# Reordering three engines inside a step of the second block's neighbourhood attention, and moving TensorE's fill to the step's end

## The reference, cut to what matters

```python
proj = h @ w_in[l]
q_lat, kv_lat, k_pe, g_mla, na_q, na_k, na_v, g_na = jnp.split(proj, split_at, axis=-1)
y_mla = _mla(...) * jax.nn.silu(g_mla)
y_na  = _na(na_q, na_k, na_v, ...) * jax.nn.silu(g_na)
h_res = h_res + jnp.concatenate([y_mla, y_na], axis=-1) @ w_out[l]
```

```python
s = concatenate([q k^T * scale + rel_bias (in the window), q k_meta^T * scale + meta_bias])
o = softmax(s) @ [v_win, v_meta]
```

## Time and profile before

| | us |
|---|---|
| median of 3 runs | 1332.66 (1331.65 to 1333.54) |
| the profiled execution, whole | 1332.1 |
| its span, first to last instruction | 1330.3 |
| TensorE matmul busy | 1257.1 (94% of the span) |
| VectorE / ScalarE / Pool busy | 822.6 / 658.1 / 152.2 |

### The profile page before, as it was taken

The page is one execution under the profiler, slowest core; times in us unless marked ns, Lnnn a source line. Parts: engine busy times, 40 slices in busy tenths (PEclk is TensorE's granted clock), DMA queues, the critical chain, the costliest instruction groups (busy, mean ns, idle before and its releaser), DMA issues.

```text
span 1330.3 us, 27430 instructions
## 1 busy us (share of the span) xinstructions
PE 1257.1 (94%) x10074; PEld 1208.1 (91%) x10074; DVE 822.6 (62%) x1378; ACT 658.1 (49%) x1105; POOL 152.2 (11%) x209
## 2 busy tenths in 40 slices
PE   6999999999999999999999999999799999976778
PEld 6999999999999999999999999999698799765667
DVE  6666655777666656666557776676666654343334
ACT  5554544455445444445445554554466566243332
POOL 3000001440000000000104400000200000043310
PEclk9999999999999999999999999999899999998888
DMA  7555644345556535556443465565244124332221
GB/s 276 190 187 191 233 162 148 124 143 200 180 188 227 191 125 185 189 189 230 165 153 123 147 197 177 186 229 185 104 138 136 49 95 151 125 109 77 95 80 64
DMA packets 56197, 210.89 MB, mean 159 GB/s; under 512 B 6672, under 2 KB 8720, under 8 KB 56000
## 3 DMA queue, kind: packets, MB, share of 16 engines
q1 hardware_dynamic: 54048, 203.45, 45.5%
q0 software_dynamic: 1936, 6.47, 1.5%
q10 hardware_dynamic: 144, 0.06, 0.0%
HBM read 208.91 MB, written 1.05 MB: 158 GB/s over the span
## 4 chain that ended last, share of the span: by engine, by line
PE 88%; DVE 5%; ACT 3%; issue 2%; DMA 0%; DVEq 0%; ACTq 0%; SPq 0%
PE bank L1056 26%; PE bank L1058 25%; PE bank L1057 25%; DVE w_lo L668 2%; PE bank L1381 2%; PE bank L1094 2%; ACT w_hi L402 2%; PE bank L1364 1%; DVE h_lo L687 1%; ACT probs_T L625 1%; PE bank L1292 1%; PE bank L1294 1%; PE bank L1293 1%; PE bank L1346 1%; PE bank L1149 0%
## 5 line engine op out<-in xcount | busy, mean ns | idle before, releaser
L1056 PE MATMUL bank<-h_hi,w_hi 128*128 128x256 f32 (+1 forms) x1992 | 573.5, 288 | 32.8 <-DVE silu_all L906 16.1
L1057 PE MATMUL bank<-h_lo,w_hi 128*128 128x256 f32 (+1 forms) x1992 | 566.6, 284 | 0.0
L668 DVE TENSOR_TENSOR w_lo<-w_raw,w_hi 128x1024 fp32r<-128x1024 f32 (+1 forms) x360 | 466.3, 1297 | 161.8 <-ACT w_hi L402 161.0
L1058 PE MATMUL bank<-h_hi,w_lo 128*128 128x256 f32 (+1 forms) x1992 | 566.2, 284 | 0.0
L402 ACT ACTIVATE w_hi<-w_raw 128x1024 fp32r<-128x1024 f32 (+1 forms) x360 | 397.8, 1109 | 94.2 <-PE bank L1058 69.9
L1056 PEld LDWEIGHTS bank<-h_hi,w_hi 128*128 128x128 f32 x1992 | 381.6, 192 | 43.1 <-issue 38.9
L1058 PEld LDWEIGHTS bank<-h_hi,w_lo 128*128 128x128 f32 x1992 | 382.7, 192 | 0.0
L1057 PEld LDWEIGHTS bank<-h_lo,w_hi 128*128 128x128 f32 x1992 | 380.0, 191 | 0.9
L1056 PE MATMUL bank<-g_hi,w_hi 128*128 128x256 f32 x832 | 230.4, 277 | 0.8 <-DVE x_res L853 0.8
L1057 PE MATMUL bank<-g_lo,w_hi 128*128 128x256 f32 x832 | 229.8, 276 | 0.0
L1058 PE MATMUL bank<-g_hi,w_lo 128*128 128x256 f32 x832 | 229.7, 276 | 0.0
(11 more groups left out here) (153 smaller groups left out, 1217.5 us busy)
## 6 DMA issues: line engine op xcount, KB each, us to landing
w_raw<-in_w SPq DMA_DIRECT2D x296, 512.0 KB, 3.3
w_raw<-in_wd SPq DMA_DIRECT2D x64, 704.0 KB, 4.1
rel_bias<-in_relbias POOLq DMA_DIRECT2D x32, 128.0 KB, 2.3
btab_sb<-in_btab POOLq DMA_DIRECT2D x1, 1536.0 KB, 10.3
x_res<-in_xT SPq DMA_DIRECT2D x2, 512.0 KB, 5.0
out_T<-x_res SPq DMA_DIRECT2D x8, 128.0 KB, 1.7
rope_sb<-in_rope POOLq DMA_DIRECT2D x1, 272.0 KB, 3.7
mats_sb<-in_mats POOLq DMA_DIRECT2D x1, 192.0 KB, 3.9
```

What stands on the lines that cost most here:

```text
L668: dve.tensor_tensor(wlo[:, slot, 0:cols], raw[:, slot, 0:cols], whi[:, slot, 0:cols].bitcast(F32), ALU.subtract).then_inc(lo_ready[slot], 1)
L1056: pe.matmul(o, h, xh, start=first, stop=False)
L1057: pe.matmul(o, h, xl, start=False, stop=False)
L1058: return pe.matmul(o, lo, xh, start=False, stop=last)
```

## The change

TensorE's step becomes scores(i), values(i-2), transposes(i-1), fill(i): the fill comes last. ScalarE's probs_T moves from behind exp(i), where it was for step i-1, to the start of step i, where it is for step i-2. VectorE makes the `w_lo` of piece i+2 in step i instead of that of piece i+3, from step 1 on. Pool issues the two DMAs of a step first, then makes both copies, then both waits and additions. The number and the sizes of all instructions stay the same, and so does the first attention's order.

```diff
-            for i in range(2 * NH):
-                h, t = 2 * (i // 4) + i % 2, i // 2 % 2
-                if i >= 4:
-                    pool.wait_ge(nm_done, U0 + 2 * MH + i - 3)
-                pool.dma_start(rel[:, i % 4, 0:T], relbias[h][:, 2 - 2 * t:6 - 2 * t, :].rearrange("p r c -> p (r c)"))\
-                    .then_inc(rel_loaded[i % 4], 16)
-                pool.tensor_copy(rel[:, i % 4, T:TM], metab[:, h, :])
-                pool.wait_ge(rel_loaded[i % 4], 16 * (i // 4 + 1))
-                r4 = rel[:, i % 4, 0:T].rearrange("p (r c) -> p r c", r=4)
-                pool.tensor_tensor(r4, r4, cmask[:].unsqueeze(1).broadcast_to([P, 4, GW]), ALU.add).then_inc(rel_ready, 1)
+            for step in range(NH):
+                t = step % 2
+                for hh in range(2):
+                    i, h = 2 * step + hh, 2 * (step // 2) + hh
+                    if step >= 2:
+                        pool.wait_ge(nm_done, U0 + 2 * MH + i - 3)
+                    pool.dma_start(rel[:, i % 4, 0:T], relbias[h][:, 2 - 2 * t:6 - 2 * t, :].rearrange("p r c -> p (r c)"))\
+                        .then_inc(rel_loaded[i % 4], 16)
+                for hh in range(2):
+                    pool.tensor_copy(rel[:, (2 * step + hh) % 4, T:TM], metab[:, 2 * (step // 2) + hh, :])
+                for hh in range(2):
+                    i = 2 * step + hh
+                    pool.wait_ge(rel_loaded[i % 4], 16 * (i // 4 + 1))
+                    r4 = rel[:, i % 4, 0:T].rearrange("p (r c) -> p r c", r=4)
+                    pool.tensor_tensor(r4, r4, cmask[:].unsqueeze(1).broadcast_to([P, 4, GW]), ALU.add)\
+                        .then_inc(rel_ready, 1)
...
             def attention(v0, steps, mla):
                 for i in range(steps + 3):
+                    if not mla and 2 <= i < steps + 2:
+                        probs_T(v0, i - 2)
...
-                    if 1 <= i <= steps:
+                    if mla and 1 <= i <= steps:
                         probs_T(v0, i - 1)
...
-                    if not mla and i < FILL:
-                        split2(FILL0 + i + LEAD)
+                    if not mla and 1 <= i <= FILL:
+                        split2(FILL0 + i - 1 + LEAD)
...
                     if i < steps:
                         scores(v0, i, mla)
-                        if not mla:
-                            fill(i)
                     if i >= 2:
                         values_of(v0, i - 2, mla)
                     if 1 <= i <= steps:
                         transposes(v0, i - 1)
+                    if i < steps and not mla:
+                        fill(i)
```

## The result

The changed kernel takes 1277.53 us (median of 4, 1277.10 to 1277.77), the kernel before 1332.16 beside it. The ratio is 0.9589, with a 95% interval of 0.9573 to 0.9606. The forecast was 1283 us with a range of 1276 to 1295. The profiled execution took 1277.69 us with a span of 1275.9, 54.4 us less than the one of before; 49.9 were forecast.

What follows compares the result with a forecast made beforehand. No engine was full; a loop of waits through TensorE, ScalarE and VectorE set the pace. Work 83.8 plus stalls 6.6 gives 90.4 for 138.9, saving 48.5, plus 1.4 in the tail: 49.9, so 1283 us (1276 to 1295).

Steps and rivals of the forecast that it cites:

- The loop: In the 16 steps, a loop of waits sets the pace; 37.2 us of gaps before fills go.
- The new stall behind the tanh: Steps 2 to 8: values wait for probs_T queued behind the tanh, 0.70 or 1.0 us each, 5.8 us in all.
- The stall before values(15): At the end of the steps, values(15) wait for probs_T(15): 0.8 us.
- The lengths of TensorE's parts: Per step at full clock: fill 3.00, values 0.81, transposes 0.81, scores 0.66 us; 83.8 us of work in all.
- Steps 9 to 15: Without a tanh, probs_T is hidden with 1.1 us to spare: no stall, bounds 0 to 0.5 us a step.
- rival B: In the steps, a chain through VectorE, Pool and ScalarE is late: 7 to 14 us, 1290 to 1297; chance 0.14.
- VectorE's part: `w_lo` one step later: VectorE stops waiting for ScalarE with the silu product behind it; no cost.
- Pool's part: Both DMAs first: additions end at 3.8 us; without it steps would last about 6.0 where they need 5.28.
- rival C: Pool's two DMAs in flight land twice as slowly: period 8.5 us, about 1330, no measurable change; chance 0.04.
- The clock: TensorE runs at full clock in the steps, as the longest gaps left are 1.0 us; 14.2 us go.
- rival D: TensorE stays at 1.2 GHz through the steps: up to 29 us more, 1361; chance 0.03.
- The tail: After the steps, the tail ran at 0.94 of full clock for 23.20 us; without gaps 1.4 us less.

Runs made afterwards that it cites:

- e3: The whole change without TensorE's part (fill stays right behind the scores), against the changed kernel: 1276.89 us, 0.9582 of the kernel before.
- e5: The whole change without ScalarE's part (probs_T stays behind the exps for step i-1), against the changed kernel: 1272.03 us, 0.9557 of the kernel before.
- e10: The changed kernel with ScalarE's copy of step i's transposes put between `w_hi` and the tanh: 1273.1 us, 0.9557 of the kernel before.
- e6: The whole change without VectorE's part (`w_lo` of piece i+3 stays in step i), against the changed kernel: 1286.02 us, 0.9658 of the kernel before.
- e2: The kernel before with only TensorE's and Pool's parts of the change added: 1293.91 us, 0.9712 of the kernel before.
- e4: The whole change without Pool's part (Pool stays unit by unit), against the changed kernel: 1297.77 us, 0.9741 of the kernel before.
- e7: The changed kernel with one unused extra tanh, about 1.0 us, behind each of the eight tanhs of a fill: 1286.5 us.
- e8: The changed kernel with two unused extra tanhs behind each of the eight tanhs of a fill: 1299.8 us.
- e1: The kernel before with only TensorE's fill moved to the step's end: 1300.03 us, 0.9756 of the kernel before.

## Why the prediction was right, point by point

*The loop.* Right. The 14 gaps of the earlier trace rows are gone, and so is the low clock. But I credited TensorE's move with it, and e3 shows no gap before a fill without that move. I also priced the stall that ScalarE's move brings and did not ask whether the move was needed; e5 and e10 show that it was not.

*The new stall behind the tanh.* Right in place and number, a little too long: 0.58 where I had 0.70 and 0.97 (0.88 once) where I had 1.0, seven of them, 5.1 us in place of 5.8. The stall before values(15) is 0.63 where I had 0.8. e5 and e10 show the cause by taking it away.

*The lengths of TensorE's parts.* This is the term that was mis-sized. I took all lengths from the old order, from one start to the next. Counted in that way, the fill is still 3.00 us (2.91 in every second step from step 8 on), but the transposes, 0.81 in the old order, where scores follow, take 0.63 ahead of the fill, as its first matmul starts before they have ended (1214.22 to 1214.85 in one step). The chain above gives the same 0.2 us to the fill, 2.83 in place of 3.03. TensorE's busy time in the stretch is 81.4 us where I had 83.8. That is 2.4 of the 4.5 us by which the saving is larger than forecast; the stalls are 0.8, and most of the rest is 1.15 us ahead of the first scores (1163.49 against 1164.64), which the change does not touch: chance of the execution.

*Steps 9 to 15.* Right: no stall in the changed kernel. The meetings of scaling and Pool's addition that rival B counted do not happen there: all 16 pairs of scalings take 0.63 or 0.64 us, as the faster one of the earlier trace rows did. In e6 they do, and a pair takes 0.94 beside an addition, which agrees with the rule of the Trainium skill on the SBUF interfaces that GpSimd shares with VectorE ("GPSIMD Engine Reference", "8. Key points"). Part of rival B's mechanism exists: e2 and e6 show a late chain through VectorE and ScalarE. What makes it late is mainly the order in their queues: the round of e2 shown above has one long pair of scalings (0.90 beside an addition), which is 0.3 of its 6.36 us. The change avoids that chain by its VectorE part.

*VectorE's part.* I wrote that it stops VectorE from waiting with the silu product behind it, and gave it no price of its own. e6 gives one, 5.9 us of the stretch with ScalarE's part there; e2 against e5 gives 20.1 without it.

*Pool's part.* Right that it binds without the change, but too cheap: I had 6.0 us a step from the median landing of 2.3, where e4 shows 6.6, and behind it the late bias holds up ScalarE's whole order. It is worth 18.4 us of the stretch when the other three are there, and 6.3 beside TensorE's alone. With it, Pool's work for a step was sized well: from the first issue to the end of the second addition it takes 3.9 us (1229.47 to 1233.36), where I had 3.8, and the median landing is 2.4, so rival C's doubled landings are not there.

*The clock.* Right, and e7 and e8 bound it for stalls of this kind; that it is 1.00 rules out rival D too. I spread the 14.2 us of low clock evenly over 14 gaps, where only 8 of them were followed by any. The rule of the Trainium skill that I weighed against the change ("TensorE: Matmul & The Clock Gate", "A second HAM failure mode: psum-queue depth-cycling") did not decide here: 0.6 to 1.0 us at each of seven steps left the clock at 1.00.

*The tail.* I gave 1.4 us. From its first matmul to the span's end it takes 24.5 us now (1251.36 to 1275.9) and took 26.0 (1304.30 to 1330.3): 1.5 less.

## What to carry to other kernels

When an engine works through a hand-written order, ask of each entry what it waits for, and what that others need stands behind it: here one tanh that waits for a fill's end costs over 5 us because a copy that could have been made 3 us before stands behind it, and moving that copy ahead cost nothing in e5 and e10. A loop of waits can be opened at several places, and opening it twice brings little (e3 is as fast as the whole change). So take the parts of a change out one by one: one of them may cost time (ScalarE's here), and the price of a part depends on which others are there. What counts then is the next loop, and it may not run through the engine that was waiting. Follow such a loop through every instruction ahead of each link in its own queue, not only through those that depend on each other.

## What the runs showed of the hardware that I had not expected

By the chain, a fill of 24 matmuls adds 3.03 us directly behind the scores (weights on 64 rows) and 2.83 behind the transposes. The loads of the fill's first weights show where the difference stands, in the changed kernel and then in e3:

```profile
1214.82 0.19 PEld L1064 LDWEIGHTS bank<-y_hi,w_hi 128*128 128x128 f32 x1
```

```profile
1216.51 0.19 PEld L1064 LDWEIGHTS bank<-y_hi,w_hi 128*128 128x128 f32 x1 [0.36 <-issue]
```

The first starts 0.27 us before the transposes end (1215.09). The second starts 0.07 us before the scores end (1216.58), after the load path has stood idle for 0.36 us. Whether that comes from the 64 rows was not tried. Nor was it why, by the chain, fills of every second step from step 8 on take 2.74 in the changed kernel.

The gap that TensorE has near 481 us (2.09 us in the kernel before, 2.29 in the changed one), between two stages that no kernel here changes, is followed by low clock in some executions and not in others. Windows from 470 to 500 us, of the kernel before and then of the changed one:

```profile
470.00:500.00 30.00, 27.91 (x223) 0.94 0.42 141
```

```profile
470.00:500.00 30.00, 27.70 (x234) 1.00 0.44 146
```

With the same instructions the first had a mean clock of 0.94 and got 223 matmuls done, the second 1.00 and 234. Such differences ahead of the changed stage moved its first scores between 1163.3 and 1168.0 us over the kernels here, so a few us between two kernels can be no more than that. With e4 and e1 (under e7 and e8 above) this is the second place where the length of a gap does not tell by itself whether the clock falls.
